# A trunk layer on one core: the memory attention's q norm applied as softmax scale, a router whose h is turned once and whose exponential comes first, and a first gather ahead of the loop of rounds

## The reference, cut to what matters

```python
def memory_cross_attention(h, mem_n, w_q, w_kv, qk_g, w_o):
    q = rms_norm((h @ w_q).reshape(b_, s_, XATTN_HEADS, XATTN_DH), qk_g[0])
    k, v = jnp.split(mem_n @ w_kv, 2, axis=-1)
    k = rms_norm(k.reshape(...), qk_g[1])
    logits = jnp.einsum('bshd,bmhd->bhsm', q, k) * (XATTN_DH ** -0.5)
    p = jax.nn.softmax(logits, axis=-1)
    return jnp.einsum('bhsm,bmhd->bshd', p, v).reshape(b_, s_, XATTN_W) @ w_o

def grouped_moe(h, router_w, router_b, w_gate, w_up, w_down):
    probs = jax.nn.softmax(h @ router_w + router_b, axis=-1)
    group_score = jnp.sum(lax.top_k(grouped, TOP_K)[0], axis=-1)   # grouped: 4 x 4
    best = jnp.argmax(group_score, axis=-1)                        # one group a token
    top_p, top_i = lax.top_k(masked, TOP_K)
    top_w = top_p / jnp.sum(top_p, axis=-1, keepdims=True)
    for e in range(N_EXPERTS):
        a = jax.nn.silu(h @ w_gate[e]) * (h @ w_up[e])
        out = out + gates[..., e:e + 1] * (a @ w_down[e])
```

## Time and profile before

| | us |
|---|---|
| runs | 707.16, 708.67 (median), 711.12 |
| profiled execution | 712.11 |
| its span | 710.3 |
| busy TensorE | 653.3 (92%) |
| busy VectorE | 510.1 (72%) |
| busy ScalarE | 427.1 (60%) |
| busy POOL | 24.3 (3%) |
| mean clock of TensorE | 0.977 of full |
| expert stage, from its first product to its last | 423.5 to 704 |

### The profile page before, as it was taken

How to read it: one execution, slowest core, us unless ns; L and a number is a source line. 1 busy time by engine, 2 the same in 40 slices (tenths; PEclk the granted TensorE clock), 3 DMA queues, 4 the chain that set the end, 5 groups by cost and what they waited for, 6 DMA issues and landing times.

```text
span 710.3 us, 8762 instructions
## 1 busy us (share of the span) xinstructions
PE 653.3 (92%) x3028; PEld 516.9 (73%) x3028; DVE 510.1 (72%) x578; ACT 427.1 (60%) x472; POOL 24.3 (3%) x14
## 2 busy tenths in 40 slices
PE   5999999999998999999979479999999999999993
PEld 4887888878776778888857467767776777677772
DVE  4544687554953548866544648998999899989995
ACT  6444637635752455355454529778877887788770
POOL 0100000400000000000000300000000000000000
PEclk9999999999998999999999769999999999999999
DMA  9945457636332346553186034999799979998941
GB/s 334 342 161 190 147 216 263 239 119 201 110 113 80 115 149 207 181 175 121 34 348 245 0 115 177 350 412 372 290 365 404 364 288 354 410 349 313 348 175 60
DMA packets 61053, 164.04 MB, mean 231 GB/s; under 512 B 4345, under 2 KB 9147, under 8 KB 52828
## 3 DMA queue, kind: packets, MB, share of 16 engines
q1 hardware_dynamic: 56432, 158.81, 61.5%
q10 hardware_dynamic: 4588, 4.80, 2.1%
HBM read 162.53 MB, written 2.64 MB: 233 GB/s over the span
## 4 chain that ended last, share of the span: by engine, by line
PE 65%; DVE 16%; issue 8%; ACT 5%; DVEq 3%; DMA 1%; POOL 0%; ACTq 0%; SPq 0%
PE ps L1439 14%; PE ps L1440 13%; PE ps L1447 13%; DVE w_lo L1219 8%; PE ps L1788 8%; PE ps L1420 4%; PE ps L1770 3%; PE ps L1818 3%; ACT w_hi L758 2%; DVEq L1365 2%; PE ps L1791 1%; PE ps L1582 1%; DVE y_lo L1342 1%; PE ps L1607 1%; DMA w_raw<-in_w_in 1%
## 5 line engine op out<-in xcount | busy, mean ns | idle before, releaser
L892 DVE TENSOR_TENSOR w_lo<-w_raw,w_hi 128x2048 fp32r<-128x2048 f32 (+2 forms) x54 | 118.4, 2211 | 56.3 <-ACT w_hi L498 55.7
L1439 PE MATMUL ps<-w_hi,act_hi 128*128 128x512 f32 (+1 forms) x304 | 120.3, 398 | 1.9 <-ACT w_hi L498 1.9
L1440 PE MATMUL ps<-w_hi,act_lo 128*128 128x512 f32 (+1 forms) x304 | 118.3, 391 | 0.0
L498 ACT ACTIVATE w_hi<-w_raw 128x2048 fp32r<-128x2048 f32 (+2 forms) x54 | 98.9, 1854 | 29.4 <-PE ps L1447 28.7
L1219 DVE TENSOR_TENSOR w_lo<-e_raw,w_hi 128x2048 fp32r<-128x2048 f32 (+2 forms) x48 | 97.4, 2063 | 9.2 <-ACT w_hi L758 9.2
L1219 DVE TENSOR_TENSOR w_lo<-w_raw,w_hi 128x2048 fp32r<-128x2048 f32 (+1 forms) x48 | 99.4, 2107 | 4.8 <-ACT w_hi L758 4.7
L758 ACT ACTIVATE w_hi<-w_raw 128x2048 fp32r<-128x2048 f32 (+1 forms) x48 | 84.3, 1767 | 1.1 <-PE ps L1791 1.0
L758 ACT ACTIVATE w_hi<-e_raw 128x2048 fp32r<-128x2048 f32 (+2 forms) x48 | 82.6, 1728 | 2.4 <-PE ps L1788 1.8
L1788 PE MATMUL ps<-w_hi,xg 128*128 128x512 f32 x236 | 75.0, 436 | 0.3 <-ACT xg L801 0.3
L1447 PE MATMUL ps<-w_lo,act_hi 128*128 128x512 f32 (+1 forms) x304 | 74.1, 386 | 0.0
L1439 PEld LDWEIGHTS ps<-w_hi,act_hi 128*128 128x128 f32 x304 | 58.5, 193 | 16.0 <-issue 4.1
(11 more groups left out here) (311 smaller groups left out, 969.3 us busy)
## 6 DMA issues: line engine op xcount, KB each, us to landing
w_raw<-in_w_in SPq DMA_DIRECT2D x32, 1024.0 KB, 5.4
w_raw<-in_w_expert_gate SPq DMA_DIRECT2D x24, 1024.0 KB, 6.9
e_raw<-in_w_expert_down SPq DMA_DIRECT2D x24, 1024.0 KB, 8.1
w_raw<-in_w_expert_up SPq DMA_DIRECT2D x16, 1024.0 KB, 6.7
e_raw<-in_w_expert_up SPq DMA_DIRECT2D x16, 1024.0 KB, 7.0
e_raw<-in_w_expert_gate SPq DMA_DIRECT2D x8, 1024.0 KB, 9.1
w_raw<-in_w_expert_down SPq DMA_DIRECT2D x8, 1024.0 KB, 7.8
w_raw<-in_w_xkv SPq DMA_DIRECT2D x4, 1024.0 KB, 5.7
```

Source lines behind the costliest of these rows:

```text
L498: A(bview(w_hi, b, blocks[b].shape), bview(w_raw, b, blocks[b].shape), ACT.Copy).then_inc(hi_done, 1)
L892: V.tensor_tensor(bview(w_lo, b, sh), bview(w_raw, b, sh), f32(bview(w_hi, b, sh)), ALU.subtract).then_inc(lo_done, 1)
L1439: MM(o, xh[:, t0 + k, i * P:(i + 1) * P], wh[:, k], start=first and k == 0, stop=False)
L1440: MM(o, xl[:, t0 + k, i * P:(i + 1) * P], wh[:, k], start=False, stop=False)
```

## The change

In the attention, q is turned as it is; its norm becomes the scale of the exponential and of the maximum (one column per head and token tile). The power is taken of the sum plus 128 times the epsilon, so the factor 128 ** -0.5 is in it. The values' block is cut into three parts that TensorE places around q's turns and the logits; its move comes after two of four exponential pairs. VectorE takes the maxima and normalisations by token tile. The output block waits for `oT_lo` half by half. ScalarE's two small loads move behind q's move.

In the router, the exponential stands ahead of the turning of h, and the division by the sum is dropped (the final weights are a ratio within a group, and comparisons don't depend on it). `h_turn` holds h in the gather's order in full precision; `h_hi` is a plain copy of it, and `h_lo` moves from POOL to VectorE, behind the first selection. Two comparisons and a maximum take the place of a subtraction and an addition, a scan that of three additions. The first selection is interleaved with the count of rounds.

On every engine, group 0's first slot gates and gather are in front of the loop of rounds, and the load of the number of rounds stands behind them; in the loop they are under If(r > 0).

```diff
# memory
+        h_turn = at("h_turn", xg_at + 8192, [P, NT, D])
# ScalarE, attention
-            act.dma_start(router_w[:], d_in["router_w"].rearrange("(t p) e -> p t e", t=KD)).then_inc(ld["moe"], 16)
-            act.dma_start(g_ffn_row[:], d_in["norm_ffn"].to_broadcast([P, D])).then_inc(ld["moe"], 16)
-            move(C_V1, *[(xkv[:, i, XW:2 * XW], acc(C_V1, i), ACT.Copy, rs_mem[:, i:i + 1]) for i in range(NT)])
+
+            act.dma_start(router_w[:], d_in["router_w"].rearrange("(t p) e -> p t e", t=KD)).then_inc(ld["moe"], 16)
+            act.dma_start(g_ffn_row[:], d_in["norm_ffn"].to_broadcast([P, D])).then_inc(ld["moe"], 16)
             for v in range(2 * NT):
+                if v == 2:
+                    move(C_V1, *[(xkv[:, i, XW:2 * XW], acc(C_V1, i), ACT.Copy, rs_mem[:, i:i + 1]) for i in range(NT)])
...
-                            ACT.Exp, scale=XDH ** -0.5, bias=x_nm[:, 2 * v + k:2 * v + k + 1],
+                            ACT.Exp, scale=rs_q[:, 2 * v + k:2 * v + k + 1], bias=x_nm[:, 2 * v + k:2 * v + k + 1],
# ScalarE, router and rounds
-            act.wait_ge(s["h_full_done"], 1)
-            A(h_hi[:].rearrange("q i (t p) -> q i t p", t=KD), h_full[:].rearrange("q i (p t) -> q i t p", t=KD),
-              ACT.Copy).then_inc(s["h_hi_done"], 1)
             act.wait_ge(s["router_max_taken"], 1)
             A(prob[:], prob[:], ACT.Exp).then_inc(s["router_exp_done"], 1)
+            act.wait_ge(s["h_full_done"], 1)
+            A(h_turn[:].rearrange("q i (t p) -> q i t p", t=KD), h_full[:].rearrange("q i (p t) -> q i t p", t=KD), ACT.Copy)
+            act.drain()
+            A(h_hi[:], h_turn[:], ACT.Copy).then_inc(s["h_hi_done"], 1)
+            for name in ("y_hi_done", "gu_moved"):
+                act.drain().then_inc(s[name], FREE)
             for n in range(2, RING):
                 e_hi(0, n)
...
-            for name in ("y_hi_done", "gu_moved"):
-                act.drain().then_inc(s[name], FREE)
+            gathered(0, range(KD))
+            act.wait_ge(s["rounds_ready"], 1)
+            rounds = act.value_load(n_rounds_i[0:1, 0:1], min_val=1, max_val=S // SLOTS)
             with act.Fori(0, rounds) as r:
-                gathered(r * NG, range(KD))
                 with act.If(r > 0):
+                    gathered(r * NG, range(KD))
# POOL
-            pool.wait_ge(s["h_hi_done"], 1)
-            nc.gpsimd.tensor_tensor(h_lo[:].rearrange("q i (t p) -> q i t p", t=KD),
-                                    h_full[:].rearrange("q i (p t) -> q i t p", t=KD),
-                                    f32(h_hi[:]).rearrange("q i (t p) -> q i t p", t=KD),
-                                    ALU.subtract).then_inc(s["h_lo_done"], 1)
# VectorE, attention
-            dve.wait_ge(*moved(C_XQ))
-            mean_square("xq", ss_q, XDH, sq_q[:].rearrange("p i (h d) -> p (i h) d", d=XDH))
+            dve.wait_ge(s_sq["xq"], 1)
+            V.reduce_sum(ss_q, sq_q[:].rearrange("p i (h d) -> p (i h) d", d=XDH), AX.X)
+            dve.drain()
+            V.tensor_scalar(ss_q, ss_q, XDH * EPS, None, ALU.add).then_inc(s_ms["xq"], 1)
             dve.wait_ge(s_rs["xq"], 1)
-            qv = xq[:].rearrange("p i (h d) -> p (i h) d", d=XDH)
-            V.tensor_tensor(qv, qv, by_row(rs_q, NT * XH, XDH), ALU.mult).then_inc(s["xq_ready"], 1)
...
-                V.tensor_scalar(nm, nm, -(XDH ** -0.5), None, ALU.mult).then_inc(s["x_max_done"], 1)
+                V.scalar_tensor_tensor(nm, nm, -1.0, rs_q[:, 2 * v:2 * v + 2], ALU.mult, ALU.mult).then_inc(s["x_max_done"], 1)
...
-            x_maxima(0)
-            x_maxima(1)
-            for v in range(2 * NT):
-                if v + 2 < 2 * NT:
-                    x_maxima(v + 2)
-                x_normalise(v)
+            for t in range(NT):
+                x_maxima(2 * t)
+                x_maxima(2 * t + 1)
+                x_normalise(2 * t)
+                x_normalise(2 * t + 1)
# VectorE, router
-            V.reduce_sum(rsum, v2(prob), AX.X)
-            dve.drain()
-            V.reciprocal(rrec, rsum)
-            dve.drain()
-            V.tensor_tensor(v2(prob), v2(prob), two(rrec, NE), ALU.mult)
-            dve.drain()
...
+            V.tensor_tensor(m4(ge), p_i, p_j, ALU.is_ge)
             V.tensor_tensor(m4(gt), p_i, p_j, ALU.is_gt)
-            V.tensor_tensor(m4(ge), p_i, p_j, ALU.is_ge)
-            dve.drain()
-            V.tensor_tensor(ge, ge, gt, ALU.subtract)
             dve.drain()
...
-            V.tensor_tensor(gt, gt, ge, ALU.add)
+            V.tensor_tensor(gt, gt, ge, ALU.max)
...
-            V.memset(earlier, 0.0)
...
-            for g in range(1, NG):
-                V.tensor_tensor(v24(earlier)[:, :, g], v24(earlier)[:, :, g - 1], v24(eq)[:, :, g - 1], ALU.add)
-                dve.drain()
-            V.scalar_tensor_tensor(first, earlier, 0.0, eq, ALU.is_equal, ALU.mult)
+            for i in range(NT):
+                V.tensor_tensor_scan(so_far[:, i * NG:(i + 1) * NG], ones[:, 0:NG], eq[:, i * NG:(i + 1) * NG], 0.0,
+                                     ALU.mult, ALU.add)
+            dve.drain()
+            V.scalar_tensor_tensor(first, so_far, 1.0, eq, ALU.is_equal, ALU.mult)
             dve.drain()
             one_group = bc(first.unsqueeze(2), (P, NT * NG, EPG))
+            V.scalar_tensor_tensor(v84(chosen), v84(rank), 2.0, one_group, ALU.is_lt, ALU.mult).then_inc(s["chosen"], 1)
             V.tensor_tensor(v84(topw), v84(r2), one_group, ALU.mult)
-            V.scalar_tensor_tensor(v84(chosen), v84(rank), 2.0, one_group, ALU.is_lt, ALU.mult).then_inc(s["chosen"], 1)
...
-            for k in range(2, S // SLOTS):
+
+            def more_rounds(k):
                 V.scalar_tensor_tensor(total[:, 1:2], total[:, 0:1], float(k * SLOTS), total[:, 1:2], ALU.is_gt, ALU.add)
-                dve.drain()
+
+            def select_tile(i, g0):
+                return V.tensor_tensor(sel[:, i], bc(iota.unsqueeze(1), (P, EPG, P)),
+                                       bc(v2(posm)[:, i, g0].unsqueeze(2), (P, EPG, P)), ALU.is_equal)
+
+            assert S // SLOTS == 4 and NT == 2
+            for i in range(NT):
+                V.tensor_copy(gcur[:, i], f32(gates_split[:, i, :, 0:EPG]))
+            more_rounds(2)
+            dve.drain()
+            select_tile(0, slice(0, EPG))
+            more_rounds(3)
+            dve.drain()
             V.tensor_copy(n_rounds_i[:], total[0:1, 1:2]).then_inc(s["rounds_ready"], 1)
-
-
-            dve.wait_ge(s["rounds_ready"], 1)
-            rounds = dve.value_load(n_rounds_i[0:1, 0:1], min_val=1, max_val=S // SLOTS)
-
+            select_tile(1, slice(0, EPG)).then_inc(s["sel_ready"], 1)
...
-            select(0, 0)
+            dve.wait_ge(s["h_hi_done"], 1)
+            for i in range(NT):
+                ins = V.tensor_tensor(h_lo[:, i, :], h_turn[:, i, :], f32(h_hi[:, i, :]), ALU.subtract)
+            ins.then_inc(s["h_lo_done"], 1)
+            slot_gates(0)
+            dve.wait_ge(s["rounds_ready"], 1)
+            rounds = dve.value_load(n_rounds_i[0:1, 0:1], min_val=1, max_val=S // SLOTS)
             dve.drain().then_inc(s["y_lo_done"], FREE)
             with dve.Fori(0, rounds) as r:
-                slot_gates(r * NG)
                 with dve.If(r > 0):
+                    slot_gates(r * NG)
# TensorE, attention
+            def values_block(part, tokens=range(NT)):
+                in_block(first_block[C_V1], act_hi, act_lo, t0=4, first=False, last=True, part=part, tokens=tokens)
+
             turn_heads(xkv, "xk_turned", 6)
-            in_block(first_block[C_V1], act_hi, act_lo, t0=4, first=False, last=True)
-
-            pe.wait_ge(s["xq_ready"], 1)
+            values_block("hi", range(1))
+            pe.wait_ge(*moved(C_XQ))
             turn_heads(xq, "xq_turned", 4)
-            pe.wait_ge(s["xq_moved"], 2)
+            values_block("hi", range(1, 2))
             pe.wait_ge(s["xk_moved"], 2)
             for t in range(NT):
                 for h in range(XH):
+                    if t == 0 and h % 2 == 0:
+                        pe.wait_ge(s["xq_moved"], h // 2 + 1)
                     ins = MM(ps[:, 4 + 2 * t + h // 2, h % 2 * S:(h % 2 + 1) * S], xqT[:, h, t * P:(t + 1) * P], xkT[:, h, :],
                              start=True, stop=True)
                     if h % 2:
                         ins.then_inc(s["x_logits_done"], 1)
+                if t == 0:
+                    values_block("lo")
             pe.wait_ge(*moved(C_V1))
             for t in range(NT):
...
-            pe.wait_ge(sL["o"], 2)
-            chunk(C_XO, oT_hi, oT_lo)
+            o_block = first_block[C_XO]
+            wh = bview(w_hi, o_block, blocks[o_block].shape)
+            pe.wait_ge(*moved(C_XO - 2))
+            pe.wait_ge(hi_done, o_block + 1)
+            for h in range(XH):
+                if h % 2 == 0:
+                    pe.wait_ge(sL["o"], h // 2 + 1)
+                for i in range(NT):
```

(18 more changed lines are left out.)

19 lines of the change are left out of this document (8 added, 11 removed).

## The result

The changed kernel took 701.03 us (median of 4 runs, 696.69 to 702.45) beside 709.67 for the kernel before: ratio 0.9859, interval 0.9822 to 0.9896. It is faster, by 8.6 us. The forecast was 15.5 us and 693.2, with 690.0 to 698.0 as its range: the sign was right, the time fell outside. A second set of six runs of the same kernel gave 697.53 and a gain of 12.0; the two medians are 55% and 77% of the forecast.

A forecast was written before the change was run, and what follows sets the result against it. It took engine-to-engine chains of short instructions, with TensorE waiting, to bound the attention and router-to-first-expert stretches ahead of a TensorE-busy expert stage. Gains 5.3 and 10.2 us: 708.67 - 15.5 = 693.2, range 690.0 to 698.0.

The forecast's parts named there:

- Attention: Memory attention: logits 3.9 us earlier, value products 4.5, output block 5.9 in all; 5.3 taken, bounds 3.6 and 5.9.
- SP's and ScalarE's moved loads: Expert loads start at 359.0 instead of 356.2, ScalarE's router weights and gain behind xqT; cost put at nothing.
- Register load: TensorE's load of the number of rounds, between first gather and first expert product: costs 0.7 us, bounds 0 and 1.2.
- rivals 3 and 4: 3: expert stream sets the pace, 695.3, chance 0.07. 4: most of the gain is given back, 706, chance 0.03.
- rival 5: Slower: TensorE stands at the skipped If before the first expert product, its code fetched behind loads; from 15.5 us; chance 0.02.
- That idleness goes: Attention: TensorE's idleness in 356 to 359 us disappears, so logits run at full clock, 1.87 us per token tile.
- the term of 1.4 for the output block: Attention's end: the output block's first eight products need only the first low half, saving 1.4 us more.
- The forecast's bound of 3.6: Attention's lower bound for the gain, 3.6 us: clock at half through the logits again, costing 1.7.
- The zero fill's end taken from the old trace: Before the places: TensorE's zero fill is late next, ends at 399.2, and places start at 399.4, 8.9 us earlier.
- rival 1: Clock stays at half in logits, places and gather: gain 12.6 us, time 696.1, chance 0.14.
- I take half the gain: First group's slot gates and gather: 2.1 us hang on the clock; half is credited, 1.0 us in the sum.
- The forecast's last sign of being wrong: The prediction is wrong if the clock is at half where it was full; no size given.

The follow-up runs named there:

- kept busy: Changed kernel plus empty identity products where TensorE waits: 693.58 us, 691.94 with the dilated attention filled too; the kernel before filled likewise: 709.67 and 706.34.
- the router's part alone: The changed kernel with the attention of the kernel before, so only router, selection and first gather changed: 703.94 us, ratio 0.9909.

## Why the prediction was wrong where it was

**Right, by its own steps.** *Attention.* Logits 4.0 us nearer to the keys' turn (3.9), the power covered, the order in the softmax as walked: value products 4.3 nearer (4.5; the column scale took 0.4 of it, and 0.1 came back from the logits). *SP's and ScalarE's moved loads*: the first expert load went out at 360.36 and no product waited for one. *Exponential* at 393.26, right behind the subtraction; no VectorE operation with 128x32 in and out over 0.2 us; the zero fill late next, with the places 0.19 behind it. *Scans* 0.24 for both (0.35 taken). *h*: the turn 3.98, the contiguous copy 1.91, as taken from the earlier trace rows; h_lo 2.34 (2.4), begun right behind the selection. *Register load*: 0.79 between the last gather product and the first expert product (0.7). *Expert stage*: 200.1 us both times, gain neither given back nor paced by the stream, which speaks against rivals 3 and 4; that TensorE's skipped If costs 0.2 at most, against rival 5. Places to slot gates was even 0.8 shorter than taken, and that is the clock as well: the places ran at its full level (0.39 for a pair of products, 0.61 before), VectorE read them 1.32 behind their start instead of 2.35, and its selection was 0.25 longer than taken.

**Wrong: the clock, in four terms.** The forecast had a right clue in hand, that the clock falls around TensorE's waits. It used it to credit time for the waits that go, 1.7 us in the logits and 1.0 in slot gates and gather, and debited nothing behind the waits that stay.

1. *"That idleness goes", for the attention.* It did go from ahead of the logits, and they had the full clock. But the wait for softmax stayed, 3.0 us idle as before, and now the clock fell behind that one. The value products lost 1.69 at the lower clock, and with them the term of 1.4 for the output block: 0.05 measured, 1.64 when kept busy. The attention brought 4.3 where 5.3 was taken: 1.0 us. Of the 1.6 by which it is under the 5.9 walked, 0.4 is the column scale, put at nothing. The forecast's bound of 3.6 has the same mechanism, but at the logits and not at the value products.
2. *The zero fill's end taken from the old trace.* While it was hidden ahead of 9 us of waiting, its length did not matter; as the step that is late next it had to be priced at either clock. Second half and fill together took 10.0 us instead of 7.3 before, 2.8 us later for the places. Kept busy they take 5.6. The rows of before (0.73 in 394 to 400) showed the clock falling inside it, and rival 1 named it but priced only places and gather. The lower clock in the second half comes with the new attention: 3.44 to the fill in all four such kernels without filling there, 1.81 to 2.52 in all five with the old one, behind the same wait of 1.6 us. So the router's part alone kept its 10.1 and lost 2.3 of it in company.
3. *"I take half the gain" in slot gates and gather.* The clock stood at 0.50 from 403 to 408, as it had before, and slot gates to first expert product took 9.15 where 8.8 was taken: 0.3 us. A full clock would not have paid the credit: in the kept-busy kernels the slot gates have it, and the stretch takes 9.45 and 9.64, since TensorE then waits 0.88 for h_lo (the forecast had 0.2).
4. *The tail.* The last down products waited 2.85 us and then ran at 0.59: 88.2 instead of 86.6, 1.6 us. Both profiles of the kernel before have the same wait and 86.6 (its variant with the exponential first has the fall). With the wait filled, the down products had the full clock in all four kept-busy profiles; in two of them (88.0 for the changed kernel, 88.5 for the one before) the fall came behind the next wait, of 2.80, in the last scatter products. No step of the forecast looked there, and why the same wait brings a fall in one kernel and not in another was not settled.

The four make 1.0 + 2.8 + 0.3 + 1.6 = 5.7 us, less the 0.8 by which places to slot gates was shorter: 4.9, which is the 15.5 of the forecast less the 10.6 by which the keys' turn to the end became shorter. The kept-busy kernels show it for the first two terms, 4.4 us and 1.6: fill the waits, change nothing else, and value products, second half and fill are back at the full clock. The whole distance is then 16.9 or 15.3 shorter than before; against the kernel before with the same filling it is 13.4 and 13.6. So the forecast of 15.5 would have been about 2 us too high even with the clock full on both sides, since 2.7 of it were credits of the clock.

**And the scale itself.** By the granted clock of each run ((1 - clock) x 2 x span), ten runs of the changed kernel spent 19 to 36 us at the lower clock, and their spans follow it with 0.47 us for each (correlation 0.97). In 71 runs of the kernel before it is 0.29 (0.64): there more of it may fall where TensorE would wait anyway, which no run separates. So the measured gain depends on where the dips fall in each execution, and the medians 8.6 and 12.0 are two draws. The forecast's last sign of being wrong, the clock at half where it was full, is what came. Rival 1, with a chance of 0.14, was nearest in kind, and half right: gather at the lower level, but logits and places at the full one, and the loss in three places that it did not price. Its 696.1 is under both medians, 701.03 and 697.53.

Two sums of the forecast don't follow from its own terms. The router's lower bound, half clock all the way and the full load, is 10.2 - 1.0 - 0.5 = 8.7 and not 9.0; the upper one, with both clock terms added, is 10.2 + 1.0 + 1.1 = 12.3 and not 11.7. The changed kernel had 7.9 there, under either lower bound, because the second half and the fill, which the bounds leave out, took 2.8 more.

What stays open: why the kernel before gains only 0.7% from the same filling though its keys' turn to the end is 1.8 to 3.5 us shorter; why the new attention brings the fall in the router's second half; and why of two equal waits one is followed by a fall and the other not. The waits and their filling were tested; what the clock's fall obeys was not found.

## What to carry to other kernels

When a wait goes, ask not only which engine is late next but at which of its two clocks it will do that work: price every TensorE step that moves onto the path at 1.2 GHz as well as at the clock of the trace, and look at the waits that stay as well as at the one that goes: a fall can come behind a wait that cost no clock before. Empty products put into waits of 1 to 3 us can pay, here 2.5 us of a stretch for 6 of them and 5.6 to 9 us of 700 for 57; in the kernel before, filling the same waits brought 0.7% or nothing. Put them only where TensorE waits anyway and where what follows is on the path. And before a gain is judged by one profile, measure from a point behind the code that did not change.

## What the runs showed of the hardware

- TensorE's lower clock outlasts the wait: with TensorE busy for 6.80 of 7 us (392 to 399, products of 128x128 and 128x16) it was granted 0.57. The same 32 products of the zero fill took 3.82 us in one kernel and 6.59 in another. A wait alone does not decide it: behind 3.1 idle of 5.7 us the value products had 1.00 in the kernel before, behind 3.0 of 5.4 in the changed one 0.66. I had not expected dips in code that two kernels share to differ by execution: 200 to 250 us had 0.90 in one profile and 1.00 in another of the same kernel.
- A POOL subtraction of 5.53 us held VectorE adds of 128x2 for all of its length; it is the meeting in time, not the size, that makes the price. Without POOL's instruction the multiply that it had held for 5.00 took 0.19.
- ScalarE's exponential of 128x256 took 0.47 us with a constant as scale and 0.56 with a column, its bias being a column in both.
- ScalarE reading every eighth element took 3.98 us for 128x2048, contiguous 1.91; VectorE's strided subtraction 3.82, contiguous 2.34 (in two instructions). Two passes on ScalarE were no slower at the end, since each fell beside other work.
